# Three projections between the modulation blocks, and three reorderings in later stages, of a one-core decoder-layer kernel

## What is computed

```python
mod = jnp.dot(jax.nn.silu(c), w_ada[l]) + b_ada[l]              # 9 rows of c, 2048 x 12288 weights
sh1, sc1, g1, sh2, sc2, g2 = jnp.split(mod[:, None, :], N_MOD, axis=-1)
h = rmsnorm(x, g_mix[l]) * (1 + sc1) + sh1
z = jnp.dot(h, w_in[l])
zq, zk, zv, zu, gq, gk, gv, gg, ga = jnp.split(z, split_idx, axis=-1)
# A) window attention on zq, zk, zv   B) causal pooling of zu   C) gated linear attention on gq, gk, gv, gg, ga
mix = jnp.concatenate([o_a, o_b, o_c], axis=-1).astype(x.dtype)
x = x + g1 * jnp.dot(mix, w_out[l])
h2 = rmsnorm(x, g_ffn[l]) * (1 + sc2) + sh2
gate, up = jnp.split(jnp.dot(h2, w_gu[l]), 2, axis=-1)
x = x + g2 * jnp.dot(jax.nn.silu(gate) * up, w_down[l])
y = rmsnorm(x, g_final)
```

## Time and profile before

| what | us |
|---|---|
| median of 3 runs (lowest, highest) | 2444.57 (2444.43, 2444.83) |
| the profiled execution | 2438.74 |
| its span, first to last instruction | 2436.6 |
| PE busy | 2321.5, 95% of the span |
| DVE busy | 1550.0 |
| ACT busy | 922.1 |

### The profile page before, as it was taken

How to read it: one execution, slowest core, us unless ns; L and a number is a source line. 1 busy time by engine, 2 the same in 40 slices (tenths; PEclk the granted TensorE clock), 3 DMA queues, 4 the chain that set the end, 5 groups by cost and what they waited for, 6 DMA issues and landing times.

```text
span 2436.6 us, 44374 instructions
## 1 busy us (share of the span) xinstructions
PE 2321.5 (95%) x18645; PEld 2173.4 (89%) x18645; DVE 1550.0 (64%) x2240; ACT 922.1 (38%) x1328; POOL 240.6 (10%) x289
## 2 busy tenths in 40 slices
PE   5689999999999999899999999999999989999996
PEld 1179888888887899899999999999999989999996
DVE  0442642333324322887888888888788878888898
ACT  2122432323233222654444444444444433333443
POOL 3150240000000111100000000000000211011131
PEclk9989999999999999999999999999999999999998
DMA  9955465655563433223433443344344676365552
GB/s 340 345 184 184 155 168 176 226 166 204 176 212 107 173 114 115 109 102 137 169 129 121 159 166 137 137 169 141 124 160 152 260 271 226 132 217 191 181 216 87
DMA packets 191078, 422.43 MB, mean 173 GB/s; under 512 B 14692, under 2 KB 116884, under 8 KB 188832
## 3 DMA queue, kind: packets, MB, share of 16 engines
q1 hardware_dynamic: 171072, 341.35, 40.8%
q0 software_dynamic: 17216, 73.78, 8.6%
q10 hardware_dynamic: 2592, 4.46, 0.5%
HBM read 365.45 MB, written 54.08 MB: 172 GB/s over the span
## 4 chain that ended last, share of the span: by engine, by line
PE 91%; DMA 3%; DVE 3%; issue 2%; ACT 1%; POOL 0%; SPq 0%; DVEq 0%; POOLq 0%; ACTq 0%
PE PJ L2327 28%; PE PS L2327 28%; PE PJ L1948 25%; DMA AR<-in_weights 3%; PE PJ L1901 2%; PE PJ L2292 1%; PE PS L2183 1%; PE PJ L1891 1%; PE PS L2292 1%; PE PJ L2269 1%; PE PJ L1913 1%; DVE X L1868 0%; PE PS L2221 0%; PE PS L2186 0%; DVE HS L1790 0%
## 5 line engine op out<-in xcount | busy, mean ns | idle before, releaser
L2327 PE MATMUL PS<-HS,WO 128*128 128x272 f32 x5376 | 686.3, 289 | 10.8 <-issue 10.1
L2327 PEld LDWEIGHTS PS<-HS,WO 128*128 128x128 f32 x5376 | 681.4, 189 | 12.3 <-issue 12.3
L2327 PE MATMUL PJ<-HS,WO 128*128 128x272 f32 x5376 | 683.0, 289 | 0.0
L2327 PEld LDWEIGHTS PJ<-HS,WO 128*128 128x128 f32 x5376 | 679.7, 188 | 0.0
L1115 ACT ACTIVATE WO<-GR 128x1024 fp32r<-128x1024 f32 (+1 forms) x462 | 477.1, 1033 | 511.7 <-PE PS L2327 246.9
L1643 DVE TENSOR_TENSOR WO<-GR,WO 128x1024 fp32r<-128x1024 f32 (+1 forms) x462 | 555.7, 1203 | 120.4 <-ACT WO L1115 120.2
L1948 PE MATMUL PJ<-HH,WH 128*128 128x272 f32 x1568 | 347.0, 303 | 18.4 <-issue 8.0
L1948 PE MATMUL PJ<-HL,WH 128*128 128x272 f32 x1568 | 327.1, 290 | 0.0
L1948 PE MATMUL PJ<-HH,WL 128*128 128x272 f32 x1568 | 325.5, 289 | 0.0
L1274 DVE TENSOR_TENSOR WL<-RW,WH 128x1024 fp32r<-128x1024 f32 x102 | 130.8, 1286 | 281.5 <-ACT WH L854 281.2
L1948 PEld LDWEIGHTS PJ<-HH,WH 128*128 128x128 f32 x1568 | 247.5, 191 | 52.7 <-issue 41.0
(11 more groups left out here) (310 smaller groups left out, 1871.7 us busy)
## 6 DMA issues: line engine op xcount, KB each, us to landing
GR<-in_weights SPq DMA_DIRECT2D x264, 512.0 KB, 6.8
AR<-in_weights SPq DMA_DIRECT2D x256, 256.0 KB, 4.5
RW<-in_weights SPq DMA_DIRECT2D x102, 512.0 KB, 4.7
HS<-act_parts POOLq DMA_DIRECT2D x91, 544.0 KB, 5.9
act_parts<-SQ SPq DMA_DIRECT2D x40, 952.0 KB, 7.0
AR<-in_weights SPq DMA_DIRECT2D x64, 512.0 KB, 5.3
MIX<-in_xT SPq DMA_DIRECT2D x1, 4352.0 KB, 17.0
X<-in_xT POOLq DMA_DIRECT2D x4, 1088.0 KB, 9.8
```

Of the source, the lines that this page charges most:

```text
L2327: mm = e.matmul(out, w[part], HS[:, HS_AT[QUARTER[i]], y, (2 * first + k) % (KT // 2), :], start=OPENS[i] and k == 0 and x == 0, stop=k == ...
```

## The change

1. **Blocks.** The 8 modulation blocks are taken in the order 0, 4, 1, 5, 2, 6, 3, 7, so that shift and scale of the first four feature tiles are there after two blocks. They use one bank of `PS` (bank 0, turned rows in bank 1) where they had two pairs of `PJ`; a block therefore waits for `rows` of the block just before it.
2. **Three projections.** k, v and q0 run unit by unit between the blocks: 30 of their 48 units (`UNITS_AT`, three at each of ten places in blocks 4 to 7), the other 18 after the last block. Their six weight tiles are loaded ahead of blocks 3 and 5. The squares of x are summed one block earlier.
3. **Halves.** q0 no longer has a half beside it; q3 has two. SP's list is rewritten for that.
4. **Heads.** `head_mod("gk")` stands ahead of the decayed queries on DVE.
5. **Mixed tiles.** The parts of `MIX` tiles 0 to 7 are made during the last projection gg1 of the last head: on ACT ahead of gg1's own evacuation, on DVE after the state updates 5 and 7.
6. **Second quarter of h2.** `plain_hi(0, 2)` and `hs_hi(1)` stand ahead of `rms(1)` on ACT, `plain_lo(0, 2)` and `hs_lo(1)` ahead of `reciprocal(1)` on DVE.

```diff
+EARLY = 8
-SUM_AT = 3
-H_AT = 5
+SUM_AT = 2
+ADA_ORDER = (0, 4, 1, 5, 2, 6, 3, 7)
+FIRST_TILES = 3
+UNITS_AT = ((4, 5), (4, 7), (5, 1), (5, 3), (5, 5), (5, 7), (6, 1), (6, 3), (7, 3), (7, 5))
...
             if n == AS:
                 sp.dma_start(MIX[:, :, :], ins["xT"]).then_inc(S["x_in"], 16)
-            if n == ADA_V * (A_FIRST - 1):
-                for t in range(RAW):
-                    load(At(t))
+            if n in (ADA_V * 3, ADA_V * 5):
+                for t in range(FIRST_TILES):
+                    load(At(t + (FIRST_TILES if n > ADA_V * 3 else 0)))
             load_ada(n)
+        for t in range(LEAD):
+            load(At(t + RAW))
         load_half(0)
         x = 0
-        for t in range(T_OUT):
-            if t >= T_W["q0"] and t % 2 == 0 and t != T_W["ga"]:
+        for t in range(LEAD, T_OUT):
+            if t >= T_W["q1"] and t % 2 == 0 and t != T_W["ga"]:
                 x += 1
                 if x < N_HB:
                     load_half(x)
             load(At(t + RAW))
...
@@ ACT, last head @@
+            if h == GH - 1:
+                a.wait_ge(S["used"], v.val(1))
+                for k in range(EARLY):
+                    a.activation(HH[:, k, :], MIX[:, k, :], ACT.Copy).then_inc(S["h_hi"], 1)
             evacuate(m, v + 1, GG[1][:, :], ACT.Silu)
...
@@ ACT, FFN @@
         affine(1)
+        plain_hi(0, 2)
+        hs_hi(1)
         rms(1)
-        plain_hi(0, 2)
         plain_hi(0, 3)
-        hs_hi(1)
...
@@ DVE, heads @@
+            head_mod("gk")
             d.wait_ge(S["exp_b"], h + 1)
...
             lo(v + (1 + LEAD))
-            head_mod("gk")
...
@@ DVE, gg1 and the output projection @@
             for b in range(4, DEC_B):
                 seq_update(b)
+                if h == GH - 1 and b % 2:
+                    for k in range(2 * (b - 5), 2 * (b - 5) + 4):
+                        mixed_lo(k)
...
-        for k in range(KT):
-            if k == 6:
+        for k in range(EARLY, KT):
+            if k == KT - 4:
                 mix_head(GH - 1)
...
@@ DVE, FFN @@
         half_residual(KT - 1, 1)
+        plain_lo(0, 2)
+        hs_lo(1)
         reciprocal(1)
-        plain_lo(0, 2)
         plain_lo(0, 3)
         norm(2)
-        hs_lo(1)
...
@@ PE @@
-        def ada_block(b, pair):
-
-            if b >= 2:
-                e.wait_ge(S["ada_rows"], b - 1)
+        def ada_block(b, side):
+
+            if b:
+                e.wait_ge(S["ada_rows"], b)
...
+        units = [(k, x) for k in range(KT - 4) for x in range(FIRST_TILES)]
 
         for b in range(A_FIRST):
-            ada_block(b, b % 2)
-            if b:
-                turn_rows(b - 1, (b - 1) % 2)
+            side = {1: [lambda b=b: turn_rows(b - 1)]} if b else {}
+            for n, (at, s) in enumerate(UNITS_AT):
+                if at == b:
+                    side.setdefault(s, []).extend(lambda x=x, k=k: first_tiles(x, k) for k, x in units[3 * n:3 * n + 3])
+            ada_block(b, side)
             if b == SUM_AT:
                 sum_x()
-        turn_rows(A_FIRST - 1, (A_FIRST - 1) % 2)
+        turn_rows(A_FIRST - 1)
+        for k, x in units[3 * len(UNITS_AT):]:
+            first_tiles(x, k)
+        for x in range(FIRST_TILES):
+            for k in range(KT - 4, KT):
+                first_tiles(x, k)
...
+            if name == "q3":
+                side = joined(ada_beside(m, b, 3, 7), {11: [lambda m=m, b=b: half_after(m, b + 1)],
+                                                       14: [lambda m=m, b=b: turn_after(m, b + 1)]})
+            elif name != "ga":
+                side = joined(side, ada_beside(m, b, 6, 11))
```

More of the change, by code:

```diff
@@ L89 @@
 T_FFN = T_OUT + 2 * KT
-ROWS = [V_W + n for n in range(4)] + [W_V[n] + x for n in W_TILES[2:] for x in range(2)]
+ROWS = [V_W, V_W + 1, W_V["q0"], V_W + 2, V_W + 3, W_V["q0"] + 1]
+ROWS += [W_V[n] + x for n in W_TILES[3:] for x in range(2)]
 ROWS += [V_U + V_U_STEP * (q // 2) + 2 * (q % 2) + x for q in range(4) for x in range(2)]
@@ L862, in evacuate, with rows @@
             a.activation(halves(dst), banks(m), func).then_inc(freed[m.mod(2)], 1)
-        def rows(step, pair):
+        def rows(step, bank):
+            src = (PS if step < A_FIRST else PJ)[:, bank, :]
             halves_made = step - A_FIRST + 1
@@ L895, in _ @@
                 a.wait_ge(S["sum_done"], 1)
-                a.activation(halves(RN0[:, :]), PS[:, 0:2, 0:HT], ACT.Sqrt, bias=eps, scale=1.0 / D)\
+                a.activation(halves(RN0[:, :]), PS[:, 2:4, 0:HT], ACT.Sqrt, bias=eps, scale=1.0 / D)\
                     .then_inc(S["rms"], 1)
-            if b >= H_AT:
-                for k in range(4 * (b - H_AT), 4 * (b - H_AT) + 4):
-                    h_hi(k)
[L901 to L905, removed]
+                for n in range(3):
+                    hi(At(n))
+            if b == A_FIRST - 2:
+                for n in range(3, 6):
+                    hi(At(n))
+            rows(b, 0)
+            if b in (3, 4, 6):
+                q = (3, 4, 6).index(b)
+                for k in range(4 * q, 4 * q + 4):
+                    h_hi(k)
+        hi(At(6))
         for k in range(KT - 4, KT):
             h_hi(k)
-        for n in range(4):
-            hi(At(n + LEAD))
+        hi(At(7))
         evacuate(At(M_W["k"]), At(3), KTT[:, :])
-        evacuate(At(M_W["v"]), At(3), VTT[:, :])
-        for n, name in enumerate(W_TILES[2:]):
+        evacuate(At(M_W["v"]), At(4), VTT[:, :])
+        hi(At(8))
+        a.wait_ge(S["used"], 6)
+        a.activation(halves(MIX[:, 0, :]), PS[:, 2:4, 0:HT], ACT.Copy).then_inc(freed[M_W["q0"] % 2], 1)
+        for n, name in enumerate(W_TILES[3:]):
             m, v = At(M_W[name]), At(T_W[name])
             hi(v + LEAD)
-            if name == "q0":
+            if name == "q1":
                 a.wait_ge(S["v_t"], 1)
@@ L932, in _ @@
             hi(v + (1 + LEAD))
+            if name == "q3":
+                rows(A_FIRST + n + 1, 2 * (m + 1).mod(2))
             if name == "ga":
@@ L1924, in ada_beside, with half_after, turn_after @@
             return {k_half: [half], k_turn: [lambda: turn_rows(b, (m + 1).mod(2))]}
+        def half_after(m, b):
+            e.wait_ge(S["ada_rows"], b)
+            ada_half(b, (m + 1).mod(2))
+        def turn_after(m, b):
+            e.wait_ge(S["mod_done"], b)
+            turn_rows(b, (m + 1).mod(2))
         def joined(*sides):
@@ L1942, in accumulate @@
         def accumulate(m, v, k):
-            out = [PJ[:, 2 * m.mod(2) + w, 0:HT] for w in range(2)]
+            out = [bank[:, 0:HT] for bank in
+                   ((PS[:, 2, :], PS[:, 3, :]) if m.base == M_W["q0"] else
+                    (PJ[:, 2 * m.mod(2), :], PJ[:, 2 * m.mod(2) + 1, :]))]
             wh, wl = (t[:, P * (k % 8):P * (k % 8) + P] for t in (WH[v.mod(HIS)], WL[v.mod(RAW)]))
```

141 lines of the change are left out of this document (83 added, 58 removed).

## The result

| | us |
|---|---|
| before, median (lowest, highest of 4) | 2444.5 (2442.1, 2444.8) |
| changed kernel, median (lowest, highest of 4) | 2542.8 (2540.8, 2544.2) |
| ratio, 95% interval | 1.0406 (1.0389 to 1.0422) |
| span of the profiled execution, before and after | 2436.6, 2540.3 |

The change makes the kernel 98 us slower. The forecast was 2520 us, 2478 to 2572.

What follows compares the result with a forecast made beforehand. The prediction took TensorE (PE), busy 95% of the span, to bound the kernel. Its terms, -21 + 94 + 15 - 8 - 5 + 0 = +75 us on the median of 2444.6, gave 2520 us, range 2478 to 2572.

Steps and rivals of the forecast that it cites:

- part 4: Start of gv0 in the heads: gk's modulation rows ready earlier remove the "issue" waits, -8 us, between 6 and 8.
- Part 2, the halves: Projections u0..gg1: 28 halves issued only when their projection starts, so PE stalls on each; +94 us, bounds 66 to 122.
- the groups of the prediction: Stalls at the halves: gq, gv0, gv1 2.7 us each; gk, gg0 4.3; gg1, u0..u3 1.7, plus 0.5 each for weight tiles.
- Part 3, the clock: PE's granted clock falls behind the new stalls at the halves: +15 us, between 0 and 45.
- one stall in three: At the 28 new stalls: share assumed to drop PE's clock, each drop costing 1.6 us, giving 15 us.
- Part 1, the blocks: Modulation blocks: 30 units of k, v and q0 fill PE's idle time; -21 us, bounds 16 to 26.
- against it: Ahead of block 3: three weight tiles load uncovered by any unit, 4.4 us charged against the blocks' gain of 26.
- Parts 4 and 5: gv0 starts sooner, -8 us; at the output projection, earlier mixed tiles shorten waits and half clock, -5 us, between 0 and 7.
- Part 6: Ahead of the FFN: the 6.1 us wait shrinks but a later chain makes PE wait again; 0, between -3 and +2.
- the one in which every stall drops the clock: Rival at the halves: clock cost 45 us in place of 15, total 2550 us; chance 0.2.
- the faster one: Rival: halves from u0 on cost nothing, so parts 1, 4 and 5 stand alone, 2411 us; chance 0.05.

Runs made afterwards that it cites:

- e3: Changed kernel with eight unneeded filler matmuls ahead of each slot of the halves from u0 on, loads still late: 2640.7 us.
- e5: Changed kernel with three unneeded filler matmuls ahead of each slot of the halves from u0 on, loads still late: 2535.7 us.
- e10: e4 with gk's modulation rows, the mixed tiles and the second quarter of h2 back in their old order: 2412.4 us, ratio 0.9879.
- e4: e1 with the second half of q3 used beside ga, so q1, q2, q3 and ga carry one each: 2400.2 us, ratio 0.982.
- e6: e4 with the modulation rows of gk back behind the decayed queries on VectorE: 2407.5 us.
- e7: e4 with the parts of the eight mixed tiles made behind gg1's evacuation again: 2403.6 us.
- e1: Changed kernel with ga taking a half in SP's list too, so halves from u0 on load one projection ahead again: 2405.4 us, ratio 0.9838.
- e2: Kernel before the change, with only the halves issued one projection later from u0 on: 2567.2 us, ratio 1.0505.
- e9: Changed kernel with each half from u0 on used two units later, except in gk, SP's list unchanged: 2474.6 us, ratio 1.0131.

## Why the forecast was right, point by point

**What bounds.** TensorE, and its waits and its clock add up to the result. In the five kernels of which the u0 stretch is shown above, 527 (or 535.5 without part 4) + waits + (1 - PEclk) x length + fillers gives the measured length within 5 us (the changed kernel: 527 + 72 + 66 = 665 for 664.6; three fillers: 527 + 18 + 13 + 106 = 665 for 660.6, the worst).

**Part 2, the halves: +94, bounds 66 to 122. 72 was measured as waits; with the clock they cost 137.** The reading of SP's list was right. In gk of head 2 the first issue of the half comes 0.6 us after the projection starts, where 0.8 was worked out for gq, and the issues take 5.1 us. In 23 of the 28 halves PE starts the fourth slot 9.4 to 10.9 us after the first issue, where I had 9.8 and 0.5 for the weight tile. The term was 22 us too large. The waits at the halves in the trace, by the groups of the prediction: 33 us in gq, gv0 and gv1 (forecast 38 with the 0.5 for each), 31 in gk and gg0 (38), 8 in gg1 and u0..u3 (18). The last group, for which I had an estimate and no row, is the largest miss. In gk of head 2 I had 4.3 + 0.5 us, and the four waits are 0.65 + 0.72 + 1.14 + 0.34 = 2.9 us. There PE reaches the half 0.4 us later than I had it, the fourth slot starts 10.4 us after the start of the projection and not 11.1, and the three slots ahead of it take 2.4 us and not 1.45, since they don't follow each other closely and the third runs at half speed. So some of the wait appears as clock. In gq of heads 1 and 2, on the other hand, the fourth slot came 13 us after the start and not 10.6; see the last section.

**Part 3, the clock: +15, between 0 and 45, and about 65 was measured.** This step failed. Its mechanism was named, its size was not, and the bound of 45 did not hold. I counted a drop as 1.6 us and gave it to one stall in three, nine in all. In the trace of the changed kernel the clock falls in 17 of the 28 halves and each fall costs 3.7 us (7.4 us at half speed). In the stretch that makes PEclk 0.90 over 664.6 us: 66 us, 2.4 us for each half. I took 1.4 us of idle time between short bursts to be harmless, because the blocks from 69.5 to 113.2 us, busy for 63% of the time, kept the clock at 0.96. The halves didn't keep it: with the fillers ahead of the same late slots it is 1.00. Nor did the wait of 2.35 us at gv0, which I took as a case for the other side, say what a single wait does. In gq of head 2 PE waits 2.04 us ahead of the first slot, which already runs at half speed, as does all that PE does in the next 10 us:

```profile
607.67 1.08 PE L1945 MATMUL PJ<-AR,CS 128*32 128x256 f32 x8 [2.04 <-DMA AR<-in_weights]
```

```profile
607.70:617.90 10.20, 8.90 (x52) 5.45 (x53) 1.22 (x1) 1.44 (x2) 1.03 (x2) 0.50 0.83 292
```

Both waits stand behind dense work of PE, and what sets them apart no run here shows.

The Trainium skill, "TensorE: Matmul & The Clock Gate", section "HAM oscillation — how this bites in real kernels", was nearer than my one in three: PE that waits for a load in each tile starts each tile throttled. The traces agree for 17 of the 28 halves, and e3 and e5 agree in that the clock is 1.00 and 0.98 once the wait is filled.

**Part 1, the blocks: -21, bounds 16 to 26; 29 was measured.** The direction and the filling are right. The 30 units are 23 us of work, and the blocks end only 6.6 us later, at 131.1 where they ended at 124.5: some 16 us of idle time were filled. Of the 6.6 us, 3.4 are there when block 4 starts (72.9 where it was 69.5), behind the three weight tiles that now load ahead of block 3; PE waits 2.5 us there, and the granted clock from 56 to 69 us is 0.61. The other 3.2 are spent in blocks 4 to 7 (58.2 us where it was 55.0, with PE busy for 52.4 of it). The failing step is "against it": I charged 4.4 us for the three tiles and 1 for the single bank, against a gain of 16 us that held the waits for these tiles already: the six tiles had been loaded among the blocks before, and 7 us of waiting for them were part of the 16. Moving them ahead of other blocks adds no byte: what three of them cost ahead of block 3, blocks 4 to 7 have less to load. That the lateness of loads no longer counts once the later blocks are bound by PE is my reading; no run moves the tiles alone. The waits for ACT's copy at L1933 are 1.4 us in all. Another 2 us are a wait of 1.0 ahead of q0 and the turn behind the last block at half clock, 1.9 us where it takes 1.1, both gone and not in my sum. The 29 us are 31.9 - 3.1 from the stages; e10, where this part is alone (and q3 has one half again), gives 30.

**Not in the sum: q3, +7.** I had counted the two halves in q3 with nothing. e4 shows 8 us.

**Parts 4 and 5, -8 and -5.** Measured 8.0 by the row of waits and 7.3 in the totals (e6), and 4.6 in the stretch (e7 against e4), 3.7 in the same stretch of the changed kernel against the one before. What was said to stay did: the wait at the very start is 2.54 us where it was 2.1, and the one at WL 1.0.

**Part 6, 0.** Right, for the reason given. The timeline of PE at the FFN (start, us, wait in brackets):

```profile
1097.46 3.25 PE L2368 MATMUL PS<-HS,WY 128*128 128x272 f32 x24 [1.25 <-DVE HS L1832]
1101.60 3.29 PE L2368 MATMUL PS<-HS,WO 128*128 128x272 f32 x24 [0.88 <-DVE WO L1846]
1109.47 4.77 PE L2368 MATMUL PS<-HS,WO 128*128 128x272 f32 x24 [4.58 <-DVE HS L1832]
...
1117.92 3.29 PE L2368 MATMUL PS<-HS,WY 128*128 128x272 f32 x24 [0.65 <-DVE HS L1832]
```

The wait of 6.1 us ahead of the third product is 1.25 now, and 4.6 us stand two products later, where `hs_lo(2)` comes late behind `reciprocal(1)`.

**The sum.** Terms, forecast and measured: blocks -21, -29; q3 0, +7; waits at the halves +94, +72; clock +15, +65; gv0 -8, -8; mixed tiles -5, -4; FFN 0, +1. That is +75 in the forecast and +104 measured, where the spans differ by 103.7 (2436.6, 2540.3) and the medians by 98. The median came out 23 us above the forecast, the clock being 50 us too small and the waits 22 too large. That it came so near is in part luck: these two errors have opposite signs, those of the blocks (8 better) and of q3 (7 worse) cancel, and the median of the kernel before lies 5.9 us above its profiled execution. Of the rivals, the one in which every stall drops the clock (2550) is nearest to what happened, in mechanism and in time, though its 45 us for the clock were too few as well; the faster one (2411) is what e1 is, once the halves are issued in time.

## What to carry to other kernels

When a list of loads is rewritten by an index, ask for every load how far ahead of its use it now stands, all the way down the loop and not only at the place that was edited: here one skipped turn at ga left 28 halves with no projection between issue and use, where they had one. If a load comes too late in each tile, price it at its wait and something for the clock: here about as much again (66 beside 72 us in the changed kernel, 59 beside 66 in e2), and half as much when the waits were shorter (24 beside 46 in e9). And where idle time is filled with work, the waits in it go whatever their cause, so a moved load is not charged against it twice. The best kernels here are the changed one with the halves ahead and one of them beside ga, 2400 us, 1.8% faster than before, with or without the reordering at the FFN.

## What the runs showed of the hardware that I had not expected

- Four short waits were enough for the clock. In gk of head 2 PE idles 0.65, 0.72, 1.14 and 0.34 us within 6 us, and from the third slot on eight matmuls of 256 columns take 1.08 us instead of 0.64. In the kernel before, in the blocks from 30 to 105 us, with single waits of up to 1.9 us between bursts of 1.05 us, that had not happened.
- Beside large transfers of another queue the urgent loads landed later. At the start of gq of head 1, GpSimd writes out 1 MB of state and reads in 1 MB. It did so before too, but nobody waited for what lay beside it. The DMA issues from 452.5 to 465.5 us (KB each, median us to landing):

```profile
AR<-in_weights SPq DMA_DIRECT2D x8, 256.0 KB, 6.7
out_gla_dec<-SD POOLq DMA_DIRECT2D x1, 1024.0 KB, 7.3
SD<-in_gla_state POOLq DMA_DIRECT2D x1, 1024.0 KB, 6.5
```

  The `AR` loads land after a median of 6.7 us there and 4.9 us in gk of head 2, and SP's eight issues take longer too, 7.8 us in gq of head 2 against 5.1 us in gk of that head above. SP's issues around the former:

```profile
599.28 0.33 SPq L587 DMA_DIRECT2D RW<-in_weights  x1
599.66 7.79 SPq L600 DMA_DIRECT2D AR<-in_weights  x8
```

  That GpSimd's transfers are the cause was not tried (no run moves them), nor which of the two, landing or issuing, makes the other slow.
- A filler matmul of float32 ident by 128 columns took 0.26 us (2.05 us for eight), as two instructions each.
